# Dense feed-forward inputs of a float32 transformer kernel: the high and low tokens as one 512-column moving operand behind the high weight, the two halves in PSUM summed by VectorE

## The reference, cut to what matters

```python
def _swiglu(h, w1, w3, w2):
    return (jax.nn.silu(h @ w1) * (h @ w3)) @ w2

x = x + _swiglu(h, ffn_w1[l // 2], ffn_w3[l // 2], ffn_w2[l // 2])
```

## Time and profile before

| what | value |
|---|---|
| runs (3) | 1904.92 us median, 1903.02 to 1912.25 |
| profiled execution, first to last instruction | 1904.3 us; no other time is shown for this execution |
| TensorE matmul busy | 1838.9 us (97%) in 13806 |
| VectorE busy | 1301.0 us (68%) |
| ScalarE busy | 1014.9 us (53%) |
| GpSimd busy | 282.7 us (15%) |
| DMA | 364.60 MB, mean 191 GB/s |

### The profile page before, as it was taken

The page is one execution under the profiler, slowest core; times in us unless marked ns, Lnnn a source line. Parts: engine busy times, 40 slices in busy tenths (PEclk is TensorE's granted clock), DMA queues, the critical chain, the costliest instruction groups (busy, mean ns, idle before and its releaser), DMA issues.

```text
span 1904.3 us, 32009 instructions
## 1 busy us (share of the span) xinstructions
PE 1838.9 (97%) x13806; PEld 1640.8 (86%) x13806; DVE 1301.0 (68%) x1405; ACT 1014.9 (53%) x1203; POOL 282.7 (15%) x161
## 2 busy tenths in 40 slices
PE   7999999999999999899999999898999999799999
PEld 7999898999899889778878888795989898579898
DVE  5988666543598866589999999775544464955543
ACT  5673345333566425377777777666433445755331
POOL 0021002524002100000000000000625100005252
PEclk9999999999999999899999999899999999799999
DMA  7432345553443235479999999444554353025451
GB/s 271 154 113 90 115 176 220 183 198 116 166 156 112 90 111 199 177 287 352 343 359 350 348 351 356 179 178 192 184 188 155 122 177 133 1 97 217 165 209 67
DMA packets 52272, 364.60 MB, mean 191 GB/s; under 512 B 5920, under 2 KB 6048, under 8 KB 9760
## 3 DMA queue, kind: packets, MB, share of 16 engines
q1 hardware_dynamic: 50832, 357.79, 50.9%
q0 software_dynamic: 1296, 4.72, 0.6%
HBM read 360.39 MB, written 2.10 MB: 190 GB/s over the span
## 4 chain that ended last, share of the span: by engine, by line
PE 56%; DVE 5%; ACT 2%; issue 2%; DMA 0%; DVEq 0%; ACTq 0%
PE banks L1342 55%; ACT work L804 1%; DVE work L3018 1%; DVE small L3022 1%; DVE more_lo L2269 1%; PE banks L1927 1%; ACT h_hi L804 0%; DVE h_lo L2318 0%; DMA ring<-weights_in 0%; PE banks L1887 0%; ACT L804 0%; DVE work L2624 0%; PE banks L2153 0%; DVE work L2621 0%; DVE ring_lo L2269 0%
## 5 line engine op out<-in xcount | busy, mean ns | idle before, releaser
L1342 PE MATMUL banks<-h_hi,ring_lo 128*128 128x256 f32 x1664 | 471.1, 283 | 0.0
L1342 PE MATMUL banks<-h_hi,high 128*128 128x256 f32 x1520 | 440.7, 290 | 6.5 <-DVE h_lo L2318 5.7
L1342 PE MATMUL banks<-h_lo,high 128*128 128x256 f32 x1520 | 431.0, 284 | 0.0
L2269 DVE TENSOR_TENSOR ring_lo<-ring,high 128x2048 fp32r<-128x2048 f32 x154 | 352.7, 2300 | 74.6 <-ACT high L804 73.1
L804 ACT ACTIVATE high<-ring 128x2048 fp32r<-128x2048 f32 x154 | 292.4, 1903 | 77.9 <-DMA ring<-weights_in 71.6
L1342 PEld LDWEIGHTS banks<-h_hi,ring_lo 128*128 128x128 f32 x1664 | 319.2, 192 | 0.0
L1342 PEld LDWEIGHTS banks<-h_hi,high 128*128 128x128 f32 x1520 | 292.3, 192 | 12.4 <-issue 7.2
L1342 PEld LDWEIGHTS banks<-h_lo,high 128*128 128x128 f32 x1520 | 292.3, 192 | 3.2 <-issue 2.9
L762 POOL CAST g_hi<-hidden 128x256 fp32r<-128x256 f32 x66 | 151.9, 2302 | 815.2 <-DVE hidden L2287 815.2
L804 ACT ACTIVATE work<-banks 128x512 f32<-128x512 f32 (+5 forms) x135 | 86.6, 647 | 260.2 <-PE banks L1342 253.1
L2269 DVE TENSOR_TENSOR more_lo<-more,more_high 128x2048 fp32r<-128x2048 f32 (+1 forms) x86 | 189.6, 2218 | 37.4 <-ACT more_high L804 36.3
(11 more groups left out here) (279 smaller groups left out, 3688.9 us busy)
## 6 DMA issues: line engine op xcount, KB each, us to landing
ring<-weights_in SPq DMA_DIRECT2D x225, 1024.0 KB, 4.9
more<-weights_in SPq DMA_DIRECT2D x104, 1024.0 KB, 5.0
more<-weights_in SPq DMA_DIRECT2D x8, 512.0 KB, 4.0
ring<-weights_in SPq DMA_DIRECT2D x6, 512.0 KB, 4.2
consts<-consts_in SPq DMA_DIRECT2D x1, 2034.0 KB, 17.2
params<-params_in SPq DMA_DIRECT2D x1, 1162.5 KB, 10.9
x<-x_in SPq DMA_DIRECT2D x2, 512.0 KB, 3.8
normed_rows<-scr POOLq DMA_DIRECT2D x2, 512.0 KB, 8.8
```

The lines of the kernel that those rows point to most:

```text
L1342: return pe.matmul(out_, lhsT, rhs, start=start, stop=stop, **kw)
L2269: tt(lo_of(g), ring_of(g), hi_of(g).bitcast(F32), SUB).then_inc(unit_lo, 1)
```

## The change: what it does

TensorE's three matmuls for each `(m, k)` become two: the high weight by high and low tokens together, one moving operand of 512 columns in two runs of 256, written to a whole bank; and the low weight by the high tokens, 256 columns, added to the first half of that bank. To this end `h_hi` and `h_lo` become halves of one tensor `h_parts`. A tile now takes two banks (`4 + 2 * (t % 2) + m`), so two tiles are in flight, and tile `t` waits for the sum of tile `t - 2`. VectorE gets a new instruction for each tile, a `tensor_reduce` that adds the two halves of both banks (1024 inputs in each partition, innermost step 256 columns, 512 outputs) to a place in `scr`; ScalarE's silu and VectorE's multiplication read that. VectorE's order becomes: sum, low parts, multiplication.

```diff
-        h_hi, h_lo = sb("h_hi", [P, KT, T], F32R), sb("h_lo", [P, KT, T], F32R)
+        h_parts = sb("h_parts", [P, 2, KT, T], F32R)
+        h_hi, h_lo = h_parts[:, 0, :, :], h_parts[:, 1, :, :]
...
+        def ffn_sum(t):
+            return grid(scr[:, 2 * T * (t % 2):2 * T * (t % 2) + 2 * T], 2)
+
+        def sums_done(name, h, t):
+            return (2 * SPLIT[name] + h) * FT + t + 1
...
@@ ScalarE, ffn_split @@
-                        act.wait_ge(unit_used, base + u + 1)
+                        act.wait_ge(glu_sums, sums_done(name, h, t))
                         act.wait_ge(glu_done, (h + FIRST_EXPERT[name]) * FT + t)
-                        f(glu[:, t % 2, :], banks[:, 4 + t % 4, 0:T], ACT.Silu).then_inc(glu_silu, 1)
+                        f(glu[:, t % 2, :], ffn_sum(t)[:, 0, :], ACT.Silu).then_inc(glu_silu, 1)
                         split_to(u + 3 + min(u, 2))
...
@@ TensorE, ffn_split @@
-                        if t >= 4:
-                            pe.wait_ge(glu_done, (h + first) * FT + t - 2)
+                        if h or t >= 2:
+                            pe.wait_ge(glu_sums, sums_done(name, h, t - 2))
                         split_ready(g)
                         for m in range(2):
-                            ins = feature_tile(banks[:, 4 + t % 4, m * T:m * T + T], g, m * P,
-                                               norm=norm if h == 0 and t == 0 and m == 0 else None)
+                            o = banks[:, 4 + 2 * (t % 2) + m, :]
+                            for k in range(KT):
+                                if h == 0 and t == 0 and m == 0 and k % 2 == 0:
+                                    pe.wait_ge(input_lo, input_part(norm, TT - 1, k // 2))
+                                w_hi, w_lo = parts_of(g, 2 * P * k + m * P, P)
+                                mm(grid(o, 2), w_hi, h_parts[:, :, k, :], k == 0, False)
+                                ins = mm(o[:, 0:T], w_lo, h_hi[:, k, :], False, k == KT - 1)
                         ins.then_inc(unit_used, 1)
...
@@ VectorE, ffn_split @@
+                        dve.wait_ge(unit_used, base + u + 1)
+                        dve.wait_ge(glu_done, first * FT + t)
+                        pair = banks[:, 4 + 2 * (t % 2):6 + 2 * (t % 2), :].rearrange("p m (c s) -> p m s c", c=2)
+                        dve.tensor_reduce(ffn_sum(t), pair, AX, ADD).then_inc(glu_sums, 1)
+                        low_to(u + 2 + min(u, 2))
                         dve.wait_ge(glu_silu, first * FT + t + 1)
-                        tt(hidden[:, t, :], glu[:, t % 2, :], banks[:, 4 + t % 4, T:2 * T], MUL).then_inc(glu_done, 1)
-                        low_to(u + 2 + min(u, 2))
+                        tt(hidden[:, t, :], glu[:, t % 2, :], ffn_sum(t)[:, 1, :], MUL).then_inc(glu_done, 1)
```

More of the change, by code:

```diff
@@ L600, in build @@
         tile_full = sem("tile_full")
-        glu_silu, glu_done = sem("glu_silu"), sem("glu_done")
+        glu_silu, glu_done, glu_sums = sem("glu_silu"), sem("glu_done"), sem("glu_sums")
         ffn_added = sem("ffn_added")
```

## The result

| what | before | after |
|---|---|---|
| median, 4 runs each | 1904.11 us | 1891.76 us (1891.7 to 1898.6) |
| ratio, 95% interval | | 0.9941 (0.9918 to 0.9964) |
| profiled execution, its own time | not shown (span 1904.3) | 1898.6 us (span 1896.8) |
| TensorE matmuls | 13806 | 12750 |

The change takes 12.3 us off, 0.6%.

A forecast was written before the change was run, and what follows sets the result against it. In the dense networks' stretches only TensorE's matmul rate was taken to count. 1056 merged matmuls give 10 us, all other terms 0, leading from the median 1904.92 to 1895 us; range 1888 to 1906.

The forecast's parts named there:

- TensorE's term: Dense networks' input halves: three 256-column matmuls become one of 512 and one of 256, 1056 times; gain set at 10 us.
- The disputed price, the wide matmul: TensorE's 512-column matmul in the input halves, priced at 0.2292 us from the output products' rows (0.2302 and 0.2283).
- "dense" gives less: First input half of "dense": narrow matmuls 0.0006 us cheaper than in "f1", so gain 0.0012 us smaller for each (m, k).
- The wait and the sum: Tile t waits for the sum of tile t - 2, taken at 1.3 us on VectorE, hidden under TensorE: cost 0.
- The strided row: VectorE operation stepping over 16 columns, 1013 ns for 480 elements; gave the sum's upper bound of 1.99 us.
- `g_lo` of tile 10: GpSimd's late `hidden`: this low part, 5.7 us after the last input tile, comes at worst at 10.5 of 22: cost 0.
- rival C: VectorE becomes the bound: strided PSUM sum takes 3.8 us, tile 6.6 us, TensorE waits every tile; 1962 us, chance 0.07.
- Rival A: The whole fixed cost comes back: wide matmul 0.2263 us, gain 13.8 us, 1891 us; chance 0.12.
- Rival B: No gain: the wide matmul's two-run operand is fed as two, at 0.2394 us or more; 1905 us, chance 0.12.
- Rival D: New wait bites in tiles 2 to 4 of first halves, sum 2 to 2.8 us: 1 to 3 us a network; 0.01.
- The formula: Skill's warm gap between matmuls, N / 2.4 + 2.5 ns: 2.6 us gain, 1902.3 us; rejected in favour of the trace.

The follow-up runs named there:

- experiment 1: The changed kernel as it is, once more, beside the kernel before on the same chip: 1891.86 us (6 runs), ratio 0.9946 (0.9933 to 0.9958).
- experiment 2: Changed kernel, but the high weight takes high and low tokens in two 256-column matmuls, the old count: 1903.75 us (12 runs), ratio 1.0004.
- experiment 6: Changed kernel with the wide matmul at 384 columns in 7 of 8 slices: 1842.91 us (4 runs), ratio 0.9673.
- experiments 4: Changed kernel, but the low weight takes only the first 128 of 256 tokens: 1887.06 us (2 runs).
- experiment 5: Three matmuls a slice as before the change, each with the first 128 tokens only: 1961.44 us in 2 runs (1931.71 and 1991.17).
- experiment 7: Changed kernel with the low weight also by high and low tokens, both matmuls 512 columns: 2009.06 us (2 runs).
- experiment 3: Changed kernel, but outside each network's first tile the 512-column operand is one contiguous run, with wrong tokens: 1889.38 us (6 runs), ratio 0.9932.
- experiment 9: Changed kernel with each tile's VectorE sum made three times: 1910.41 us (8 runs), ratio 1.0034.
- experiment 8: Changed kernel with each tile's VectorE sum made twice: 1899.1 us (10 runs), ratio 0.9983.

## Why the prediction was right

**The result.** 1895.0 us was forecast, with a range from 1888 to 1906, and 1891.76 measured; the runs beside it moved the kernel before as well, from 1904.92 to 1904.11. The gain of 10 us against 12.3 (11.8 in experiment 1, whose interval gives 8 to 13 us) came from the step that was named for it, as experiment 2 shows.

**TensorE's term.** It was right in its sum, and in its parts by luck. Forecast 0.0092 to 0.0102 us for each of 1056. Measured by the stages: "f1" 3.79 us less over 352 slices of m and k, 0.0108; "dense" 2.25 us, 0.0064; "f0" (63.21 and 63.17 before, 61.46 and 61.23 after) 3.69 us, 0.0105. That makes 9.7 us in all. So the sum of the stages is the forecast's, and the medians show 2 to 2.6 us more than the stages hold. That remainder is within the interval. Stages that the change leaves alone scatter by more than that between executions: from the second output products of "f0" to the start of "f1" the traces have 233.6 us before, 235.2 in experiment 2, and for the changed kernel 241.6 in its first profile and 232.0 in experiment 1. From three or four runs of each kernel one can't say that the 2 us are more than this.

**The disputed price, the wide matmul.** I took 0.2292 from the output products' rows, and in the first half of "f1" it was 0.2316; the narrow one that stays came out at 0.1174 and not at its 0.1197. The two errors, 0.0024 up and 0.0023 down, cancel, and the pair of 0.3489 us was met to 0.0001. That is luck: nothing in the prediction has a narrow matmul cheaper beside a wide one. By the numbers of this half the merge itself gives back 2 x 0.1199 - 0.2316 = 0.0082 us, and the narrow one that stays gives the other 0.0025. Why it does is not shown. The picture behind the number, a fixed cost beside the columns, was half right. It holds between 384 and 512 columns (0.0165 and 0.018 us, experiment 6). At 256 columns the matmul stands just above the least time of 0.112 us for a matmul with its weight load (experiments 4 and 5). Had the matmuls been of 128 columns, the same merge would by these numbers have paid far more for each: two of 0.112 become one of 0.120.

**"dense" gives less** than the others, 1.1 to 1.2 us a half against 1.9. I had seen that its narrow matmuls ran faster and took 0.0012 off for it, from a window that ended 0.1 us behind the stage; measured it was 0.0044 less than "f1". Its narrow ones stood at 0.1190 before, where those of "f1" stood at 0.1197, and its wide ones stand at 0.2325 and 0.2327 in the two halves, where those of "f1" stand at 0.2316 and 0.2305. Why stays open; no run was made for it.

**The wait and the sum.** Forecast cost 0, measured 0 (experiment 2, and the unchanged waits of "f1"). The sum was bounded by 1.22 and 1.99 us and taken at 1.3; it is 1.225. The strided row that set the upper bound was the wrong neighbour. Two small slips in the prediction's working change nothing: `g_lo` of tile 10 is there 6.2 us after the last tile, not 5.7, and rival C's surplus over 5.75 us is 0.85, not 0.87.

**Rival A** (0.2263 for the wide one) is out as a mean: over whole halves of the changed kernel it is 0.2305 to 0.2327. Single distances do come down to 0.226, and in experiment 7 those behind one buffer of the weight in "f0" average 0.227. **Rival B** (no gain, two runs fed as two) is out by experiment 3. **Rival C**: its mechanism is real and was made to happen in experiment 9. A sum of 3.8 us, as C had it, was not run. Its tile was too long: by distances it is 3.8 + 2.20 + 0.34 = 6.3 us and not 6.6. At experiment 9's tile of 5.93 us C's rule, a tile's surplus times 66, gives 66 x (5.93 - 5.58) = 23 us, and 18.6 were measured. The rule is near in total and not in its parts, since the first halves lost 5.4 us each and the second ones 1.0. In a steady tile VectorE binds from about 3.0 us a sum, not from 2.8. **Rival D** (a sum of 2 to 2.8 us delays a few tiles of each first half) was made to happen in experiment 8, with sums of 2.35 us: 0.3 to 0.7 us in each network, below the 1 to 3 it was priced at, and at the start of tile 5, not in tiles 2 to 4.

The Trainium skill ("Advanced Engine Details and Errata", section PSUM Cachelines) wants every two consecutive elements in PSUM contiguous for best throughput. This does not show in a VectorE read: 1.225 us with a step of 256 columns, 1.220 for as many contiguous ones in SBUF.

**The formula** of the Trainium skill, N / 2.4 + 2.5 ns ("TensorE: Matmul & The Clock Gate", section Back-to-back issue gap), gave 2.6 us of gain, and the runs gave 12. The prediction left out that the same section keeps the formula for an isolated matmul and says that in a stream of weight loads and matmuls both set the spacing. That section of the Trainium skill puts the spacing at about 81 ns for 128 columns and 131 ns for 512; here the traces have 112 and 232 ns, so they do not agree with these figures either. The Trainium skill, on the same page in section LDWEIGHTS, puts a weight load at its columns / 1.2 GHz, by which 128 columns are 107 ns. At the full clock the least time measured here, 0.112 us, agrees; at the lower level it was 0.213, twice the Trainium skill's figure.

**What was not forecast:** the profiled execution's extra 6.8 us. TensorE's clock stood at its lower level for more time in the mixer between "f0" and "f1". From 1560 to 1640 us the mean clock is 0.74, and 0.83 in the same stretch of the kernel before, whose row is the second:

```profile
1560.00:1640.00 80.00, 69.01 (x496) 59.20 (x497) 45.80 (x88) 44.32 (x95) 0.00 (x0) 0.74 0.21 80
...
1560.00:1640.00 80.00, 69.65 (x541) 59.96 (x540) 47.11 (x84) 41.48 (x86) 0.00 (x0) 0.83 0.29 105
```

TensorE has gaps there in both (69.01 and 69.65 of 80 us busy). From the second output products of "f0" to the start of "f1" the changed kernel's first profile has 48 us at the lower level, the kernel before 31, and experiment 1 has 27. The runs with the same kernel and mean clocks of 0.982 and 0.983 took 1891.7, the one with 0.979 took 1898.6. This scatter between executions is over half of the gain looked for, so the stages' own lengths were the better measure in this study.

## What to carry to other kernels

Where TensorE streams one matmul after another, measure the distance between starts at both widths: twice the narrow one less the wide one is what a merge of two matmuls behind one weight pays (0.008 us here, and 0.0025 more because the matmul beside it got cheaper). The least time of a matmul with its weight load (0.112 us) tells where widening pays much more. An added VectorE sum and a shorter PSUM rotation were free here as long as the helper's tile, taken from distances and not from durations, stayed under TensorE's, tiles with double work counted in; doubling and tripling the added work shows how far away that edge is. For a change of half a per cent, compare the lengths of the stages it touches, and undo the one part that should carry the gain.

## What the runs showed of the hardware that was not expected

- In a stream of matmuls of 128 columns, each with its own weight load, each takes 0.112 us at the full clock and 0.213 us at the 1.2 GHz level; 256 columns take 0.1197 and 0.2138. At the lower level half of the columns save nothing.
- What a matmul costs beside its columns (at 2.4 GHz) is not one number: 0.0165 us at 384 columns, 0.018 at 512, but 0.011 to 0.013 at 256.
- Two experiments had streams of 128-column matmuls with TensorE shown busy without a gap. In experiment 5, with all matmuls narrow, the first halves of "dense" and "f0" ran at the lower clock for nearly their whole length, and the four other halves, with the same stream, at the full clock; the kernel came out 28 and 88 us slower than before with half of the columns gone. In experiment 4, where wide ones stood between, no half did. What decides between the two was not tried.
- A wait of TensorE that its matmuls' rows hide can stand in the rows of its weight loads: 6.5 us against 2.7 in experiment 9, where the stage was 6.8 us longer.
